# First spectrum step ahead of the ctx square sums, and adaLN blocks 11 to 15 mixed one k step later

## The chip, the cores and the metric

The kernel runs on one core of a Trainium2 chip. The metric is the device time of one execution in microseconds. "Before" is the kernel as it stands, "after" the kernel with the change. Engines are named as in the profile: PE is TensorE (PEld its weight loads), ACT is ScalarE, DVE is VectorE, POOL is GpSimd and SP is SyncE. SP and POOL issue transfers from queues of their own.

## The reference

One layer of a hybrid backbone over 512 latent tokens and 256 context tokens of 2048 channels. Only its first part matters here:

```
mod  = silu(c)     @ w_ada + b_ada     # 6 x 2048, the first 4096 columns are shift and scale of the mixer
modc = silu(c_ctx) @ w_ada + b_ada
h_x  = rms_norm(x + pos, g) * (1 + scale) + shift        # latents
h_c  = rms_norm(ctx, g) * (1 + cscale) + cshift          # context
u_c  = h_c @ w_in[:, :1024]
p_x  = h_x @ w_in                                        # split into u, Hyena v/x0/x1, gates
taps = window * filter_mlp(positions)                    # 1024 channels, forward and backward
kf   = spectrum of taps                                  # used much later, by the long convolution
```

After it come the S5 scan, the long convolution, the gated merge, the output projections and a SwiGLU feed-forward layer, which the change doesn't touch.

## The kernel before

Tensors are stored with channels on the 128 partitions, so that D = 2048 gives KT = 16 tiles of channels. Every engine has a program of its own, and semaphores order them. The order of work on each engine is written out by hand. The change concerns the first 180 us, in which four strands are interleaved.

**Coefficients (ada blocks 0 to 15).** Block c gives shift and scale of channel tile c, for x and for ctx. SP loads it (`ada_mix(c)` on SP, 2 MB, three buffers, so the load of block c waits for the end of the matmuls of block c - 3). PE multiplies it (`ada_mix(c)` on PE, 32 records of 128x256), ACT copies the result to SBUF (`ada_rows(c)`), PE turns the rows into columns (`mix_columns(c)`, four small matmuls), and DVE makes the coefficients (`mix_coefficients(c)`). PE's `ada_mix(c)` waits until DVE has the coefficients of block c - 2, since both use one of two PSUM banks.

**Norms.** ACT squares the ctx tiles and then the x tiles into four buffers (`square(k)`), and PE sums each with a matmul by ones (`sums(k)`), which frees the buffer. From the sums come the reciprocal roots `rs_x` and `rs_c`.

**Filter spectrum.** `taps(t)` makes four tiles of taps (PE, then DVE: s_tap counts finished tiles). Eight steps `spectrum_of_filter(st)` on PE (8 records of 128x512 each) are folded by DVE (`filter_fold(st)`, kf_free counts them) and stored to HBM by POOL. The fold of step st waits for the store of step st - 2.

**First products.** `weights(n)` on SP loads slice n of w_in (0.5 MB) into slot n % 3. ACT makes the high part (`split_hi(n)`), DVE the low part (`split_lo(n)`), and `units_by_k(k)` on PE does 24 matmuls for channel tile k with slice k // 2, into PSUM banks 0 to 5. It needs tile k of h, which DVE scales (`block(k)`: x, ctx, and the two low parts) and ACT completes (`h_hi_tile(k)`, `hc_hi_tile(k)`). Slot 1 lies over a buffer of the folds, so `weights(1)` waits for kf_free = 8, the last fold.

SP's queue is strict. Its order around the change is:

```
weights(0), ada_mix(11), weights(2), ada_mix(12), ada_mix(13), [kf_free 8] weights(1),
ada_mix(14), ada_mix(15), weights(3), weights(4), ...
```

After the 16 steps of `units_by_k` the kernel goes on with products for the other columns of w_in.

Of the kernel before, what the change touches and what calls it, by code (L numbers as in the profile page):

```python
# [22 lines left out]
KT = D // P  # L23
# [100 lines left out]
def block_kernel(nc, vecs_d, w_ac_d, w_ar_d, w_in_d, w_glu_d, w_hy_d, w_out_d, w_fi_d, w_fo_d, x_d, ctx_d,  # L124
# [363 lines left out]
    with nc.Block() as block:  # L488
# [375 lines left out]
        def _(act):  # L864
# [43 lines left out]
            def ada_rows(c):  # L908

                act.wait_ge(am_used, c + 1)  # L910
                act.activation(arow[c % 2][:, :], ps[6 + c % 2][:, 0:2 * P], ACT.Copy).then_inc(am_row, 1)
# [27 lines left out]
            for st in range(8):  # L939
                if 1 <= st < 5:  # L940
                    for k in range(KT + 4 * st - 4, KT + 4 * st):
                        square(k)
                if st == 4:
                    act.wait_ge(s_squ, 2 * KT)
                    act.activation(ssr[:, 0:SEQ], ps[4][:, :], ACT.Copy)
                    act.activation(ssr[:, SEQ:SEQ + CTX], ps[5][:, 0:CTX], ACT.Copy).then_inc(s_row, 1)
                if 2 <= st < 7:
                    ada_rows(3 + st)
                if st == 5:
                    act.wait_ge(s_var, 1)  # L950
                    act.activation(rt6[:, 2, :], rt6[:, 1, :], ACT.Sqrt).then_inc(s_sqrt, 1)
                if st == 6:
                    act.wait_ge(s_rsp, 1)
                    act.activation(rs_x[:, :], ps[5][:, :], ACT.Copy).then_inc(s_rs, 1)
                    act.activation(rs_c[:, :], ps[4][:, 0:CTX], ACT.Copy).then_inc(s_rs, 1)
                if st == 7:
                    h_hi_tile(0)
                    hc_hi_tile(0)
                    split_hi(0)
                    ada_rows(10)  # L960
                    ada_rows(11)
            for k in range(KT):
                if k < KT - 1:
                    h_hi_tile(k + 1)
                    hc_hi_tile(k + 1)
                if k == 0:
                    act.wait_ge(kf_free, 8)
                if k < 2:
                    split_hi(k + 1)
                if k < 4:  # L970
                    ada_rows(12 + k)
                if k >= 3 and k % 2 == 1:
                    split_hi(k // 2 + 2)

# [424 lines left out]
        def _(dve):  # L1399
# [36 lines left out]
            def position(k):  # L1436

                if k % 4 == 0:
                    dve.wait_ge(s_x[k // 4], 16)
                add_position(x_raw, postab, k).then_inc(s_xp, 1)  # L1440
# [29 lines left out]
            def mix_coefficients(c):  # L1470

                dve.wait_ge(am_cmb, c + 1)
                ins = tt(md[:, c, :], ps[6 + c % 2][:, 2 * P:2 * P + 4], vecs[:, V_B4 + 4 * c:V_B4 + 4 * c + 4], ADD)
                link(ins)
                ts(mu[:, c, :], md[:, c, 2:4], 1.0, vecs[:, V_NM + c:V_NM + c + 1], ADD, MUL).then_inc(c_mod, 1)
                dve.wait_ge(c_mod, c + 1)
# [28 lines left out]
            def filter_fold(st):  # L1505

                b = st % 2
                dve.wait_ge(kf_ps, st + 1)
                if st >= 2:
                    dve.wait_ge(kf_out[b], 16 * (st // 2))  # L1510
                even, odd = ps[2 * b][:, :], kf_odd[b][:, :]
                link(dve.tensor_copy(odd, ps[2 * b + 1][:, :]))
                tt(kfs[b][:, 0, :], even, odd, ADD)
                tt(kfs[b][:, 1, :], even, odd, SUB).then_inc(kf_free, 1)
# [8 lines left out]
            mix_coefficients(3)  # L1523
            for j in range(4):
                position(j)
            mix_coefficients(4)
            a, b, c, e, r = (rt6[:, j, :] for j in range(5))
            for st in range(8):
                if 1 <= st < 4:
                    for k in range(4 * st, 4 * st + 4):  # L1530
                        position(k)
                if st == 5:
                    dve.wait_ge(s_ss, 1)
                    link(ts(a, ps[4][:, 0:6], 1.0 / D, EPS, MUL, ADD))
                    dve.reciprocal(b, a).then_inc(s_var, 1)
                if st == 7:
                    dve.wait_ge(s_rs, 2)
                    block(0)
                    split_lo(0)
                filter_fold(st)  # L1540
                if st >= 3:
                    mix_coefficients(2 + st)
                if st == 5:
                    dve.wait_ge(s_sqrt, 1)
                    link(tt(e, c, c, MUL))
                    link(tt(e, e, a, MUL))
                    link(ts(e, e, -0.5, 1.5, MUL, ADD))
                    link(tt(r, e, c, MUL))
                    dve.wait_ge(s_id, 16)
                    for j in range(6):  # L1550
                        ts(dg[:, j, :], ident[:, :], rt6[:, 4, j:j + 1], None, MUL).then_inc(s_dg, 1)
            mix_coefficients(10)
            for k in range(KT):
                if k < KT - 1:
                    block(k + 1)
                if k == 0:
                    mix_coefficients(11)
                if 2 <= k < 6:
                    mix_coefficients(10 + k)
                if k < 2:  # L1560
                    split_lo(k + 1)
                if k >= 3 and k % 2 == 1:
                    split_lo(k // 2 + 2)
# [818 lines left out]
        def _(pe):  # L2382
# [18 lines left out]
            def sums(k):  # L2401

                pe.wait_ge(s_sq, k + 1)
                bank, w = (5, CTX) if k < KT else (4, SEQ)
                mm(ps[bank][32 * (k % 4):32 * (k % 4) + 1, 0:w], ones[:, 0:1], sqr[k % 4][:, 0:w], start=k % KT < 4,
                   stop=k % KT >= KT - 4, skip_group_check=True, tile_position=(0, 32 * (k % 4))).then_inc(s_squ, 1)
# [27 lines left out]
            def mix_columns(c):  # L2434

                pe.wait_ge(am_row, c + 1)
                for v in range(2):
                    ins = mm(ps[6 + c % 2][:, 2 * P + 2 * v:2 * P + 2 * v + 2], arow[c % 2][:, P * v:P * v + P],
                             vecs[:, V_SEL:V_SEL + 2], start=True, stop=True)
                ins.then_inc(am_cmb, 1)  # L2440

            def spectrum_of_filter(st):

                cs, f, half = 1 - st // 4, st // 2 % 2, st % 2
                if st % 4 == 0:
                    pe.wait_ge(s_tabf[cs], 16)
                if st >= 2:
                    pe.wait_ge(kf_free, st - 1)
                for t in range(4):
                    ins = mm(ps[2 * (st % 2) + t // 2][:, :], tab_f[cs][:, t, P * f:P * f + P],  # L2450
                             (taps_s, taps_d)[cs][:, t, 512 * half:512 * half + 512], start=t % 2 == 0, stop=t % 2 == 1)
                ins.then_inc(kf_ps, 1)
# [24 lines left out]
            taps(3)  # L2477
            mix_columns(3)
            ada_mix(4)
            for k in range(KT):  # L2480
                sums(k)
            mix_columns(4)
            pe.wait_ge(s_tap, 4)
            for st in range(8):
                if st == 5:
                    pe.wait_ge(s_row, 1)
                    for j in range(6):
                        ins = mm(ps[4][:, j:j + 1], ssr[:, P * j:P * j + P], vecs[:, V_SEL:V_SEL + 1], start=True, stop=True)
                    ins.then_inc(s_ss, 1)
                spectrum_of_filter(st)  # L2490
                if st >= 3:
                    mix_columns(2 + st)
                if 1 <= st < 5:
                    for k in range(KT + 4 * st - 4, KT + 4 * st):
                        sums(k)
                if st >= 2:
                    ada_mix(3 + st)
                if st == 6:
                    for j in range(6):
                        pe.wait_ge(s_dg, j + 1)  # L2500
                        out = ps[5][:, P * j:P * j + P] if j < 4 else ps[4][:, P * (j - 4):P * (j - 4) + P]
                        ins = mm(out, ones[:, :], dg[:, j, :], start=True, stop=True)
                    ins.then_inc(s_rsp, 1)
# [17 lines left out]
                if k % 2:  # L2521
                    ins.then_inc(w_used, 1)

            ada_mix(11)
            mix_columns(10)
            pe.wait_ge(kf_free, 7)
            for k in range(KT):
                units_by_k(k)
                if k < 5:
                    mix_columns(11 + k)  # L2530
                if k < 4:
                    ada_mix(12 + k)

            def half_unit(n, out, xh, xl, k0, first, last, nk=ST, each=None):

# [238 lines left out]
            for j in range(4):  # L2774
                n = N_HU + j
                pe.wait_ge(w_lo, n + 1)
                for kk in range(4):
                    k = 4 * j + kk
# [14 lines left out]
            for j in range(4):  # L2793
                n = N_HU + 4 + j
                pe.wait_ge(w_lo, n + 1)
                for kk in range(4):
                    i = 4 * j + kk
                    k = K_ORDER[i]
# [288 lines left out]
```

## Time and profile before

| | |
|---|---|
| median of 3 runs | 2776.26 us (2775.99 to 2779.75) |
| profiled execution | 2771.29 us, span 2769.5 us |
| PE busy in the span | 2726.0 us (98%) |
| DVE, ACT, POOL busy | 2170.0, 1138.4, 367.6 us |
| moved by DMA | 475.27 MB, mean 172 GB/s |
| span, 0 to 140 us | PE busy 116.7 us of 140 |

The busy time of PE is modelled from pipelined matmuls, so it shows where PE is idle, not that it is at its peak. Times in the rows below are microseconds from the start of the span.

### The profile page before, as it was taken

What the parts mean: (1) busy time and instruction counts of PE and PEld (TensorE: products, weight loads), DVE (VectorE), ACT (ScalarE), POOL (GpSimd) and SP (SyncE); (2) the same over time, 40 slices, a digit from 0 to 9 for tenths busy, and PEclk for the clock granted to TensorE, in tenths of its full rate; (3) what the DMA queues carried; (4) which work ended last, traced back from release to release, by engine and by line L of the source; (5) the groups of instructions that cost most, each with busy time, mean ns of one, the idle gap of its engine ahead of it and who ended that gap; (6) DMA issues with size and microseconds to landing.
All of it is one profiled execution on the core that took longest, in us unless ns stands there. A gap on an engine that the chain in (4) does not pass through costs nothing.

```text
span 2769.5 us, 39538 instructions
## 1 busy us (share of the span) xinstructions
PE 2726.0 (98%) x15566; PEld 2312.1 (83%) x15566; DVE 2170.0 (78%) x2984; ACT 1138.4 (41%) x1697; POOL 367.6 (13%) x540
## 2 busy tenths in 40 slices
PE   7999999999999999999999999999999999999997
PEld 2688888887888888888888888888888888998996
DVE  6556676987785686676789999999999887877877
ACT  4332333223443532222245555555555554453541
POOL 0001331001333100011100111111111111000001
PEclk9999999999999999999999999999999999999999
DMA  9736884336776645767644444444443336434432
GB/s 403 324 98 157 193 188 140 121 122 197 224 224 185 238 137 184 243 210 268 232 147 146 155 145 152 142 152 147 148 154 123 126 111 218 139 91 148 138 104 95
DMA packets 144540, 475.27 MB, mean 172 GB/s; under 512 B 24993, under 2 KB 29489, under 8 KB 140130
## 3 DMA queue, kind: packets, MB, share of 16 engines
q1 hardware_dynamic: 85858, 301.43, 33.2%
q0 software_dynamic: 49760, 157.67, 18.0%
q10 hardware_dynamic: 8736, 13.63, 1.4%
q8 instruction: 124, 2.03, 0.3%
q14 instruction: 62, 0.51, 0.1%
HBM read 428.14 MB, written 44.44 MB: 171 GB/s over the span
## 4 chain that ended last, share of the span: by engine, by line
PE 90%; DMA 5%; DVE 3%; ACT 2%; issue 1%; POOL 0%; ACTq 0%; SPq 0%; DVEq 0%; POOLq 0%
PE ps L2837 19%; PE ps L2541 12%; PE ps L2543 11%; PE ps L2542 11%; PE ps L2839 10%; PE ps L2887 3%; PE ps L2888 3%; PE ps L2886 3%; PE ps L2865 2%; PE ps L2866 2%; PE ps L2867 2%; PE ps L2558 2%; PE ps L2518 1%; DMA hw_raw<-in_w_in 1%; DMA kf<-kf_st 1%; PE ps L2585 1%
## 5 line engine op out<-in xcount | busy, mean ns | idle before, releaser
L1408 DVE TENSOR_TENSOR hw_lo<-hw_raw,hw_hi 128x1024 fp32r<-128x1024 f32 x220 | 269.2, 1224 | 316.3 <-ACT hw_hi L868 315.3
L868 ACT ACTIVATE hw_hi<-hw_raw 128x1024 fp32r<-128x1024 f32 x220 | 232.6, 1059 | 672.8 <-DMA hw_raw<-in_w_in 456.4
L2837 PE MATMUL ps<-t_hi_lo,wx_hi 128*128 128x512 f32 x1312 | 412.4, 396 | 0.0
L2107 DVE TENSOR_TENSOR wx_lo<-wx,wx_hi 128x1024 fp32r<-128x1024 f32 x287 | 351.5, 1225 | 41.4 <-ACT wx_hi L1262 36.9
L2541 PE MATMUL ps<-h_hi,hw_hi 128*128 128x512 f32 x896 | 354.2, 395 | 0.2 <-DVE st_c L1672 0.2
L2543 PE MATMUL ps<-h_hi,hw_lo 128*128 128x512 f32 x896 | 349.6, 390 | 0.0
L2542 PE MATMUL ps<-h_lo,hw_hi 128*128 128x512 f32 x896 | 349.0, 389 | 0.0
L1262 ACT ACTIVATE wx_hi<-wx 128x1024 fp32r<-128x1024 f32 x287 | 302.3, 1053 | 105.3 <-PE ps L2839 99.4
L2837 PE MATMUL ps<-h_hi_lo,wx_hi 128*128 128x512 f32 x984 | 309.3, 396 | 0.0
L2839 PEld LDWEIGHTS ps<-t_hi_lo,wx_lo 128*128 128x128 f32 x1312 | 246.8, 188 | 57.8
L2839 PE MATMUL ps<-t_hi_lo,wx_lo 128*128 128x256 f32 x1312 | 257.8, 278 | 0.0
L2839 PEld LDWEIGHTS ps<-h_hi_lo,wx_lo 128*128 128x128 f32 x984 | 185.1, 188 | 43.3
L1311 ACT ACTIVATE dw_hi<-dw 128x768 fp32r<-128x768 f32 (+1 forms) x192 | 144.4, 753 | 160.4 <-PE ps L2867 129.4
L2837 PEld LDWEIGHTS ps<-t_hi_lo,wx_hi 128*128 128x128 f32 x1312 | 199.7, 189 | 0.0
L2161 DVE TENSOR_TENSOR dw_lo<-dw,dw_hi 128x768 fp32r<-128x768 f32 (+1 forms) x192 | 162.0, 845 | 47.6 <-ACT dw_hi L1311 46.7
L2541 PEld LDWEIGHTS ps<-h_hi,hw_hi 128*128 128x128 f32 x896 | 168.3, 188 | 36.5 <-issue 2.2
L2543 PEld LDWEIGHTS ps<-h_hi,hw_lo 128*128 128x128 f32 x896 | 168.2, 188 | 35.7
L2542 PEld LDWEIGHTS ps<-h_lo,hw_hi 128*128 128x128 f32 x896 | 168.4, 188 | 33.7
L2839 PE MATMUL ps<-h_hi_lo,wx_lo 128*128 128x256 f32 x984 | 193.3, 278 | 0.0
L2888 PE MATMUL ps<-blk_lo_hi,dw_lo 128*128 128x256 f32 x672 | 190.4, 283 | 0.0
L2887 PE MATMUL ps<-blk_lo_hi,dw_hi 128*128 128x256 f32 x672 | 190.4, 283 | 0.0
L2886 PE MATMUL ps<-blk_lo_hi,dw_hi 128*128 128x256 f32 x672 | 190.3, 283 | 0.0
(429 smaller groups left out, 5667.0 us busy)
## 6 DMA issues: line engine op xcount, KB each, us to landing
wx<-in_w_fi SPq DMA_DIRECT2D x164, 512.0 KB, 3.5
hw_raw<-in_w_in SPq DMA_DIRECT2D x128, 512.0 KB, 4.6
ada1m<-in_w_ar POOLq DMA_DIRECT2D x96, 512.0 KB, 4.5
ada_mix<-in_w_ac SPq DMA_DIRECT2D x16, 2048.0 KB, 12.8
dw<-in_w_fo SPq DMA_DIRECT2D x80, 384.0 KB, 3.1
ada1g<-in_w_ar POOLq DMA_DIRECT2D x32, 512.0 KB, 5.5
hw_raw<-in_w_glu SPq DMA_DIRECT2D x32, 512.0 KB, 4.7
hw_raw<-in_w_out SPq DMA_DIRECT2D x32, 512.0 KB, 4.4
```

The lines of the kernel that those rows point to most:

```text
L868: act.activation(hw_hi[slot(n)][:, :], hw_raw[slot(n)][:, :], ACT.Copy).then_inc(w_hi, 1)
L1262: act.activation(wx_hi[o % 4][:, :], wx[x_buffer(p, j)][:, :], ACT.Copy).then_inc(w_hi, 1)
L1408: tt(hw_lo[s][:, :], hw_raw[s][:, :], hw_hi[s][:, :].bitcast(F32), SUB).then_inc(w_lo, 1)
L2107: tt(wx_lo[b][:, :], wx[b][:, :], wx_hi[o % 4][:, :].bitcast(F32), SUB).then_inc(w_lo, 1)
L2541: mm(out, wh(k), xh[:, k0 + k, :], start=first and k == 0, stop=False)
L2542: mm(out, wh(k), xl[:, k0 + k, :], start=False, stop=False)
L2543: ins = mm(out, wl(k), xh[:, k0 + k, :], start=False, stop=last and k == nk - 1)
L2837: mm(out[:, :], wh[:, P * k:P * k + P], both[:, :, k, :], start=opens and k == 0, stop=False, skip_group_check=True)
L2839: ins = mm(out[:, 0:CW], wl[:, P * k:P * k + P], xh[:, k, :], start=False, stop=k == ST - 1, skip_group_check=True)
L2886: mm(out, wh[:, w], b_hi[j][:, k, :], start=opens and k == 0, stop=False, skip_group_check=True)
L2887: mm(out, wh[:, w], b_lo[j][:, k, :], start=False, stop=False, skip_group_check=True)
L2888: ins = mm(out, wl[:, w], b_hi[j][:, k, :], start=False, stop=k == K_S - 1, skip_group_check=True)
```

## The change

On PE, `spectrum_of_filter(0)` now comes ahead of the sixteen `sums(k)` of ctx and of `mix_columns(4)`. On DVE, `filter_fold(0)` comes ahead of `mix_coefficients(4)` and of the loop over the steps.

The sequence of ada blocks in the loop over k moves. Before, PE did `ada_mix(11)` and `mix_columns(10)` ahead of the loop, then after step k the columns of block 11 + k and the product of block 12 + k. Now columns 10 follow step 0, columns 9 + k follow steps 2 to 6, and the product of block 10 + k follows steps 1 to 5, so that block 11 comes behind units 1 and block 15 behind units 5. ACT's `ada_rows` and DVE's `mix_coefficients` move with them. The program of SP is unchanged, but its loads of blocks 14 and 15 wait for the ends of the products of blocks 11 and 12.

```
# ACT
                     split_hi(0)
                     ada_rows(10)
-                    ada_rows(11)
             for k in range(KT):
...
-                if k < 4:
-                    ada_rows(12 + k)
+                if 2 <= k < 7:
+                    ada_rows(9 + k)
                 if k >= 3 and k % 2 == 1:
                     split_hi(k // 2 + 2)
# DVE
             for j in range(4):
                 position(j)
+            filter_fold(0)
             mix_coefficients(4)
...
-                filter_fold(st)
+                if st:
+                    filter_fold(st)
...
-            mix_coefficients(10)
             for k in range(KT):
                 if k < KT - 1:
                     block(k + 1)
-                if k == 0:
-                    mix_coefficients(11)
-                if 2 <= k < 6:
-                    mix_coefficients(10 + k)
+                if k == 1:
+                    mix_coefficients(10)
+                if 3 <= k < 8:
+                    mix_coefficients(8 + k)
                 if k < 2:
                     split_lo(k + 1)
# PE
             ada_mix(4)
-            for k in range(KT):
-                sums(k)
-            mix_columns(4)
             pe.wait_ge(s_tap, 4)
             for st in range(8):
...
                 spectrum_of_filter(st)
+                if st == 0:
+                    for k in range(KT):
+                        sums(k)
+                    mix_columns(4)
...
-            ada_mix(11)
-            mix_columns(10)
             pe.wait_ge(kf_free, 7)
             for k in range(KT):
                 units_by_k(k)
-                if k < 5:
-                    mix_columns(11 + k)
-                if k < 4:
-                    ada_mix(12 + k)
+                if k == 0:
+                    mix_columns(10)
+                if 2 <= k < 7:
+                    mix_columns(9 + k)
+                if 1 <= k < 6:
+                    ada_mix(10 + k)
```

## Rows read from the trace of the kernel before

**Rows 1.** The page: busy time, share of the span, instructions.

```profile
PE 2726.0 (98%) x15566; PEld 2312.1 (83%) x15566; DVE 2170.0 (78%) x2984; ACT 1138.4 (41%) x1697; POOL 367.6 (13%) x540
```

**Rows 2.** Windows: stretch, length, busy by engine, PE clock, DMA share, GB/s.

```profile
59.00:111.10 52.10, 49.90 (x416) 27.11 (x415) 27.39 (x62) 13.70 (x27) 5.01 (x7) 1.00 1.01 426
...
120.00:138.00 18.00, 17.22 (x147) 13.43 (x146) 9.24 (x22) 5.92 (x10) 1.10 (x2) 1.00 0.16 55
```

**Rows 3.** The chain of waits, 96 to 117 us: start, length, what.

```profile
98.34 0.61 DVE kf_st L1514
98.96 12.12 DMA hw_raw<-in_w_in
111.16 1.07 ACT hw_hi L868
...
116.29 0.47 PE ps L2518
```

**Rows 4.** SP's issues, 90 to 113 us (x2: first issue to second).

```profile
90.19 7.48 SPq L499 DMA_DIRECT2D ada_mix<-in_w_ac  x2
98.96 0.33 SPq L509 DMA_DIRECT2D hw_raw<-in_w_in  x1
101.38 7.39 SPq L499 DMA_DIRECT2D ada_mix<-in_w_ac  x2
112.84 0.33 SPq L509 DMA_DIRECT2D hw_raw<-in_w_in  x1
```

**Rows 5.** PE in order of time, 99 to 135 us (idle before, its releaser).

```profile
99.41 1.91 PE L2429 MATMUL ps<-ada_mix,silu_c 128*2 128x256 f32 x32 [2.13 <-DVE mul_mix L1475]
...
101.72 0.48 PE L2518 MATMUL ps<-h_hi,hw_hi 128*128 128x512 f32 x1
...
106.05 0.50 PE L2438 MATMUL ps<-vecs,ada_row 128*128 128x2 f32 x4
...
108.31 0.51 PE L2518 MATMUL ps<-h_hi,hw_hi 128*128 128x512 f32 x1
...
116.29 0.47 PE L2518 MATMUL ps<-h_hi,hw_hi 128*128 128x512 f32 x1 [1.30 <-DVE hc_lo L1496]
...
122.81 0.50 PE L2518 MATMUL ps<-h_hi,hw_hi 128*128 128x512 f32 x1
...
134.90 0.47 PE L2518 MATMUL ps<-h_hi,hw_hi 128*128 128x512 f32 x1 [0.78 <-DVE hc_lo L1496]
```

**Rows 6.** Tile views: ada block issued at 97.34, then slice issued at 139.3.

```profile
DMA to landing us min/median/max: 12.5/12.5/12.5
...
DMA to landing us min/median/max: 3.7/3.7/3.7
```

**Rows 7.** PE and DVE in order of time, 41 to 57 us.

```profile
42.93 5.83 PE L2405 MATMUL ps<-sqr,ones 128*1 128x256 f32 x32 [3.45 <-ACT sqr L898]
49.16 7.11 PE L2450 MATMUL ps<-taps_dif,tab_f 128*128 128x512 f32 x16
...
41.72 0.68 DVE L1459 TENSOR_TENSOR taps_dif<-window,window 128x512 f32<-128x512 f32 x1
```

**Rows 8.** PE's clock: windows (clock third from last), then tap matmuls.

```profile
43.43:46.00 2.57, 2.57 (x16) 0.60 (x14) 0.99 (x2) 2.41 (x8) 0.00 (x0) 0.50 0.99 414
...
46.50:48.50 2.00, 2.00 (x15) 0.51 (x12) 1.01 (x2) 2.00 (x8) 0.00 (x0) 1.00 0.98 410
...
14.61 3.78 PE L2417 MATMUL ps<-f3w,fh 64*128 64x512 f32 x8 [5.22 <-ACT fh L884]
...
21.04 1.99 PE L2417 MATMUL ps<-f3w,fh 64*128 64x512 f32 x8 [0.41 <-DVE window L1448]
```

**Rows 9.** Slice 3's split to the coefficients behind it: the chain, then DVE.

```profile
129.87 0.96 ACT hw_hi L868
...
134.36 0.41 DVE hc_lo L1496
...
134.86 0.23 DVE L1475 TENSOR_SCALAR mul_mix<-mod_mix,vecs 128x2 f32<-128x2 f32 x1
```

## The prediction

> **What bounds the kernel now.** I read the page first. TensorE is busy for 98% of the span [rows 1], so most of the program is bound by it, and a change in the first 150 us pays only if it lets TensorE reach the long dense part sooner; after 140 us its idle time is small waits on neighbours, none on a clock of its own, so I pass any shift on to the end in full. Next I read the first 140 us by stretches. From 59 to 111 us all 16 DMA engines are full (share 1.01, 426 GB/s); from 120 to 138 us they are nearly empty (0.16) [rows 2]. So this stage has two limits, a DMA one until about 111 us and a TensorE one behind it. The chain of waits shows where they meet: the fold of the last spectrum step ends at 98.95, weight slice 1 is issued at 98.96, lands 12.12 us later at 111.1, and through its split on ACT and DVE and the scaling of the third h tile it releases units_by_k(2) at 116.29 [rows 3]. Last I read SP's issues [rows 4] and TensorE's order [rows 5] around that point.
>
> **Why slice 1 lands when it does.** SP issues ada block 13 at 97.34 (the second of the pair that begins at 90.19), slice 1 at 98.96 [rows 4]. Block 13 lands 12.5 us after its issue, at 109.8; slice 1 lands 1.3 us later [rows 3, 6], which is its own 0.52 MB at 426 GB/s (1.2 us). It was therefore not waiting for its issue but for the bytes ahead of it. Whoever issues it a microsecond or two sooner only lengthens its time in the queue.
>
> **Edit 1, spectrum step 0 ahead of the 16 sums of ctx squares.** TensorE reaches this place at 39.48 and waits 3.45 us for the first square [rows 7]. Step 0 needs the fourth tap tile, whose last subtraction ends on DVE at 42.40 [rows 7]. So the wait does not go; it ends 0.4 us sooner, on DVE. Step 0 takes 3.56 us (7.11 for two, rows 7) and ends at 46.0. Only four square buffers exist, so ACT squares four tiles and then stands until the sums start; the other twelve go at the present pace, 5.83/16 = 0.36 us each [rows 7], to 50.4. With its columns step 1 then starts near 51.5 in place of 52.7: 1.2 us sooner. If the low clock seen in this place [rows 8] catches step 0, it lasts up to 1.8 us longer and the gain is a loss of up to 0.6 us. Folds 0 and 1 and their stores to HBM move 2 to 6 us forward, which takes away DVE's waits for the stores; those bytes must be moved all the same before slice 1 lands. So either way ada_mix(10) ends between 96.1 and 97.9 instead of 97.28, and slice 1 is issued between 97.7 and 99.5, while block 13 is still ahead of it. Value of edit 1: nothing, covered by the full DMA engines. Were they not full it would be worth its 1.2 us.
>
> **Edit 2, ada blocks 11 to 15 one or more k steps later.** Before the first units TensorE now waits 2.13 us for the coefficients of block 9, then does ada_mix(11) and mix_columns(10) [rows 5]. Both leave, so units_by_k(0) starts near 96.1 rather than 101.72. A step of units takes 4.33 us, one mix_columns with one ada_mix 2.26 us (106.05 to 108.31), a whole round 6.52 us (116.29 to 122.81) [rows 5]. New order: units 0 to 100.4, mix_columns(10), units 1 to 105.2, ada_mix(11) to 107.1 (108.9 if step 0 was slow). Then units 2 stands until slice 1 is there. In DVE's queue the block for tile 2 still stands behind the low part of slice 1, and both follow its landing as now: 116.3. The 5 us won ahead become a wait of 7 to 9 us.
>
> What then follows is longer. Before 116.3 the kernel now has ada_mix(12) and (13) done; the new one has them still to do. **Term 1**: two rounds of 2.26 us, 4.5 us more behind the wait. The 0.78 us wait before units 5 at 134.90 [rows 5] has ACT standing at ada_row 15 ahead of the split of slice 3; that order goes, so minus 0.8. Term 1 is 3.7 us.
>
> **Term 2, the queues it is moved past.** SP's order is block 14, block 15, slice 3. Block 15's load waits for the end of ada_mix(12), because there are three buffers; now it goes out at 108.4 (with block 14 in the 101.38 row) and slice 3 at 112.84, long before it is needed [rows 4]. In the new order ada_mix(12) ends only after units 2; call that moment T (122.8 at full clock). At T block 15 goes out (2.1 MB), then slice 3. A slice alone lands in 3.7 us [rows 6]; block 15 ahead of it adds 2.1 MB / 426 GB/s = 4.9 us. I take slice 3 at T + 8.7 us. Units 3, columns 12, ada_mix(13), units 4 keep TensorE until T + 6.5 + 4.3 = T + 10.8. What follows is mix_columns(13), which waits for ada_row 13, queued on ACT behind the split of slice 3 and h_hi of tile 5; and ada_mix(14), which waits for coefficient 12, queued on DVE behind the low part of slice 3 and tile 5's block. Now, from the start of such a split (129.87) to the end of the coefficients behind the block (134.86 + 0.23) it is 5.2 us [rows 9]. So ada_mix(14) starts at T + 8.7 + 5.2 + 0.1 = T + 14.0 and units 5 at T + 15.9; without the wait T + 13.0. Term 2 is 2.9 us. Bounds: nothing if slice 3 came 3 us sooner; 4.5 us if the pair shares the engines badly (now, behind other loads, slice 1 took 12.1, three more than I give slice 3).
>
> The Trainium skill, "DMA: Bandwidth & Descriptors", section "Anatomy of one DMA — SWDGE (gpsimd) path", fits one DMA as about 2.0 us plus its bytes at 436 GB/s, for issues from GpSimd. By it slice 3 would land at about T + 8.0, term 2 would be 2.2 us and the whole sum 7.8. The row of a lone slice on this queue (3.7 us, of which its bytes are 1.2) shows 2.5 us fixed, and I go by the row.
>
> **Term 3, the clock.** An idle TensorE for 3.45 us at 39.5 was followed by a granted clock of 0.50 from 43.4 to 46.0 and 1.00 from 46.5 [rows 8], that is 1.2 and then 2.4 GHz. What the lower level costs is seen in the tap matmuls: eight of them took 3.78 us after 5.2 us idle and 1.99 us later [rows 8], 1.8 us lost. The new wait of 7 to 9 us is longer than both, units 2 is dense work behind it, so I put 1.9 us; from nothing (the 2.13 us and 1.30 us waits of rows 5 lowered nothing) to 3.7 us, twice the tap row, if it stays low for longer or falls again in the wait of term 2.
>
> **Sum.** 3.7 + 2.9 + 1.9 = 8.5 us. The profiled execution took 2771.29 us, its span 2769.5; with the change 2779.8. The median of the runs stands 5.0 us above the profiled one, at 2776.26, so I predict 2784.8 us, 0.31% slower. Below 0.2% (5.6 us) a difference is what a measurement of this kernel can't tell from none.
>
> **Rivals.**
> (a) Only term 1: the clock stays or recovers at once and slice 3 comes in time. 2776.3 + 3.7 = 2780.0, no change that counts. For it: the 2.13 us wait left the clock alone, DMA is empty by T. Against it: the long wait is four times that one.
> (b) Faster: slice 1 is bound by its issue and by the stores, not by the queue. With folds and stores 2 to 6 us sooner it would land sooner, and TensorE would run dense from 51.5 on: 1.2 + 2.13 + 1.30 + 0.78 = 5.4 us less, 2770.9. Its place is the landing of slice 1. Units 2 can follow ada_mix(11) at 107.1 only if slice 1 lands at 102; to be even with the present kernel it has to come about 7 us sooner, by 104, since terms 1 and 2 stay. For it: the chain of waits does run through the stores and the folds. Against it: block 13 is ahead of it and the engines were full all the way [rows 2, 6].
> (c) Worse: slice 3 late by its upper bound and a clock that falls twice, 3.7 + 4.5 + 3.7 = 11.9 us, 2788.2.
>
> **Numbers.** Forecast 0.70, rival (a) 0.15, (b) 0.07, (c) 0.08. The likeliest case's own range is 5.6 to 11 us, 2781.9 to 2787.3. To hold 8 in 10 I reach down to (a) less 1 us and up to (c), as the runs themselves lie between 2775.99 and 2779.75: 2779.0 to 2788.5. Slower 0.78 (forecast and (c)), within 0.2% 0.15, faster 0.07.
>
> **What the new profile would show.** Spectrum step 0 released by DVE's tap at 42.4, not by ACT. Units 0 near 96 to 98. A TensorE idle of 7 to 9 us ended by the hc_lo of tile 2 near 116, the landing of slice 1 within a microsecond of 111, granted clock 0.5 behind it. Slice 3 issued near 123 to 125 in place of 112.8, and a second idle of 2 to 3 us before mix_columns(13) or ada_mix(14). The last units step ending 8 to 9 us later than now. The prediction is wrong if slice 1 lands well before 108, if the second wait is missing, or if a later part of the kernel takes the 8 us back.

## The result, and the profile after

The changed kernel takes 2787.95 us (median of 6 runs, 2785.46 to 2790.32) against 2776.25 us before (6 runs). The ratio is 1.0036, with a 95% interval of 1.0026 to 1.0046: 0.36% slower, 11.7 us between the medians. The predicted 2784.8 us is 3.2 us short of it. The measured time lies within the range of 2779.0 to 2788.5, but near its upper end, above the likeliest case's own 2781.9 to 2787.3.

The profiled execution of the changed kernel has a span of 2786.3 us, 16.8 us over that of before. The first stage accounts for 12.2 of them. I read its end off the first matmul of the products behind the sixteen steps of units, first before and then after (PE in order of time):

```profile
180.74 0.39 PE L2558 MATMUL ps<-h_hi,hw_hi 128*128 128x512 f32 x1
```

```profile
192.91 0.39 PE L2559 MATMUL ps<-h_hi,hw_hi 128*128 128x512 f32 x1
```

Most of the other 4.6 us lies between 1000 and 1500 us. The waits there, from the view of who waited for whom, first before and then after:

```profile
PE ps L2769 <- DVE hw_lo L1408: 2.1, 2, 1.5
PE ps L2541 <- DVE hw_lo L1408: 0.6, 2, 0.4
```

```profile
PE ps L2542 <- DVE hw_lo L1407: 3.0, 7, 1.2
PE ps L2770 <- DVE hw_lo L1407: 2.1, 2, 1.5
PE ps L2542 <- DVE xacc L1955: 1.0, 2, 0.8
```

These are 2.7 us before and 6.1 after, but 7.3, 5.1 and 5.3 us in the profiles of e1, e2 and e8 below, which the change touches in part or in another form. So their number varies between executions whatever the edit. The profiled execution of before had few of them, and was 5.0 us faster than its own median. So spans are a poor measure of this change; below I read the end of the stage, and the medians of the runs beside it.

The first stage of the changed kernel. The chain of waits up to the wait of PE, to be held beside [rows 3]:

```profile
98.59 0.61 DVE kf_st L1513
99.22 13.18 DMA hw_raw<-in_w_in
112.48 1.06 ACT hw_hi L868
...
117.54 0.77 PE ps L2519
```

SP's issues, beside [rows 4]:

```profile
90.65 7.48 SPq L499 DMA_DIRECT2D ada_mix<-in_w_ac  x2
99.22 0.33 SPq L509 DMA_DIRECT2D hw_raw<-in_w_in  x1
108.70 17.53 SPq L499 DMA_DIRECT2D ada_mix<-in_w_ac  x2
126.28 4.35 SPq L509 DMA_DIRECT2D hw_raw<-in_w_in  x2
```

PE in order of time, beside [rows 5] and [rows 7]:

```profile
42.55 5.40 PE L2450 MATMUL ps<-taps_dif,tab_f 128*128 128x512 f32 x8 [3.05 <-DVE taps_dif L1458]
...
97.67 0.50 PE L2519 MATMUL ps<-h_hi,hw_hi 128*128 128x512 f32 x1
...
106.73 1.91 PE L2429 MATMUL ps<-ada_mix,silu_c 128*2 128x256 f32 x32
...
117.54 0.77 PE L2519 MATMUL ps<-h_hi,hw_hi 128*128 128x512 f32 x1 [8.90 <-DVE hc_lo L1495]
123.50 0.50 PE L2438 MATMUL ps<-vecs,ada_row 128*128 128x2 f32 x4
123.93 1.91 PE L2429 MATMUL ps<-ada_mix,silu_c 128*2 128x256 f32 x32
...
130.10 0.50 PE L2438 MATMUL ps<-vecs,ada_row 128*128 128x2 f32 x4
...
139.71 0.61 PE L2438 MATMUL ps<-vecs,ada_row 128*128 128x2 f32 x4 [2.83 <-ACT ada_row L911]
140.65 2.65 PE L2429 MATMUL ps<-ada_mix,silu_c 128*2 128x256 f32 x32 [0.34 <-DVE mul_mix L1474]
...
148.40 0.50 PE L2438 MATMUL ps<-vecs,ada_row 128*128 128x2 f32 x4
```

Windows (PE clock third from last, then DMA share and GB/s), beside [rows 2] and [rows 8]:

```profile
59.00:111.10 52.10, 49.64 (x391) 27.27 (x389) 26.24 (x58) 14.05 (x28) 5.01 (x7) 1.00 1.01 419
117.50:121.00 3.50, 3.46 (x11) 3.02 (x12) 3.07 (x5) 1.37 (x4) 0.00 (x0) 0.50 0.00 0
121.00:123.00 2.00, 2.00 (x12) 1.74 (x11) 1.65 (x4) 0.79 (x3) 0.00 (x0) 0.95 0.00 0
140.65:145.00 4.35, 4.35 (x37) 2.47 (x38) 2.48 (x6) 2.45 (x4) 0.00 (x0) 0.62 0.02 4
145.00:148.00 3.00, 3.00 (x18) 2.54 (x18) 2.47 (x4) 0.94 (x2) 0.00 (x0) 0.98 0.01 3
```

What to see: units 0 starts at 97.67 in place of 101.72, four microseconds sooner, and all of it and more is lost in the 8.90 us in which PE waits for tile 2, which hangs on slice 1. Slice 1 was issued at 99.22, 0.26 us later than before, and landed at 112.4. Units 2 then runs at a granted clock of 0.50 for its first 3.5 us. Slice 3 goes out at 126.28 in place of 112.84, and a second wait of 2.83 and 0.34 us follows, again with the low clock behind it.

The second wait in the chain of waits of the changed kernel:

```profile
126.28 8.88 DMA hw_raw<-in_w_in
135.18 1.07 ACT hw_hi L868
...
139.78 0.40 DVE hc_lo L1495
...
140.28 0.24 DVE mul_mix L1474
...
140.65 2.65 PE ps L2429 x32
```

### The profile page after: what moved, and what is told of

It reads as the page before. It is cut to its first block, busy times and chain, and to the rows that moved or that the text cites. A ratio compares the mean times of both kernels' runs of the same rounds, so it can differ in the third digit from the quotient of the medians.

```text
span 2786.3 us, 39538 instructions
## 1 busy us (share of the span) xinstructions
PE 2731.9 (98%) x15566; PEld 2312.4 (83%) x15566; DVE 2169.8 (78%) x2984; ACT 1138.1 (41%) x1697; POOL 367.5 (13%) x540
## 4 chain that ended last, share of the span: by engine, by line
PE 89%; DMA 4%; DVE 4%; ACT 2%; issue 1%; POOL 0%; ACTq 0%; SPq 0%; DVEq 0%; POOLq 0%
PE ps L2838 19%; PE ps L2542 11%; PE ps L2544 11%; PE ps L2543 11%; PE ps L2840 10%; PE ps L2889 3%; PE ps L2888 3%; PE ps L2887 3%; PE ps L2866 2%; PE ps L2868 2%; PE ps L2867 2%; DMA hw_raw<-in_w_in 2%; PE ps L2559 2%; PE ps L2519 1%; PE ps L2450 1%; DMA hw_raw<-in_w_glu 1%
```

## The experiments

"Stage end" is the start of the first matmul behind the sixteen units steps, 180.7 us before and 192.9 in the changed kernel. Ratios are to before, from runs on the same chip; they are estimated over the single runs and can differ by a few hundredths of a per cent from the quotient of two medians.

| kernel | units 2 starts | stage end | median us | ratio (95%) |
|---|---|---|---|---|
| before | 116.29 | 180.74 | 2776.25 | |
| changed | 117.54 | 192.91 | 2787.95 | 1.0036 (1.0026 to 1.0046) |
| e1, edit 1 alone | 116.14 | 180.66 | 2776.03 | 1.0002 (0.9993 to 1.0011) |
| e2, edit 2 alone | 115.99 | 191.52 | 2787.14 | 1.0041 (1.0027 to 1.0055) |
| e3, changed, slice 3 ahead | 116.35 | 186.64 | 2781.62 | 1.0018 (1.0009 to 1.0027) |
| e4, changed, slice 1 ahead | 111.83 | 188.53 | 2781.35 | 1.0017 (1.0008 to 1.0027) |
| e5, before, slice 1 ahead | 115.53 | 180.14 | 2777.19 | 1.0002 (0.9993 to 1.0011) |
| e6, changed, both ahead | 111.41 | 182.22 | 2777.26 | 1.0000 (0.9991 to 1.0009) |
| e7, changed, wait filled | 115.98 | 190.49 | 2785.07 (one) | |
| e8, rebuilt | 111.29 | 177.64 | 2773.01 | 0.9987 (0.9978 to 0.9996) |
| e9, e8 with SP's old order | 116.53 | 185.50 | 2780.74 | 1.0008 (0.9998 to 1.0017) |
| e10, e8 with edit 1 | 112.00 | 178.65 | 2774.05 | 0.9988 (0.9979 to 0.9997) |

### e1 and e2: each edit alone

e1 is the kernel before with this part of the change; e2 is the changed kernel without it.

```
# DVE
+            filter_fold(0)
             mix_coefficients(4)
# PE
-            for k in range(KT):
-                sums(k)
-            mix_columns(4)
...
                 spectrum_of_filter(st)
+                if st == 0:
+                    for k in range(KT):
+                        sums(k)
+                    mix_columns(4)
```

> The kernel before with edit 1 alone (spectrum step 0 and its fold ahead of the ctx square sums). My theory: slice 1 is bound by the bytes ahead of it in the full DMA engines, so units step 2 starts within 1.3 us of 116.3 and the last units step ends within 1.5 us of the 180.7 of before; time within 0.1% of before (2774.5 to 2778). Rival (the edit pays where slice 1 is bound by its issue): units step 2 at 115 or sooner and 1 to 3 us less. Rival (edit 1 is itself part of the loss, as slice 1 landed 1.3 us later in the changed kernel): 1 to 2 us more.

> The changed kernel with edit 1 undone, so edit 2 alone. My theory: edit 2 is the whole loss; slice 1 lands near 111 to 112.4, units step 2 starts at 116.3 to 117.5 after an idle of 7 to 9 us, the first matmul of the columns after the units steps starts 11 to 12.5 us later than the 180.7 of before; time 2786 to 2789. Rival (both edits are needed for the loss): 6 us more than before or less.

Edit 1 is worth nothing: stage end 180.66 against 180.74. Its chain of waits shows slice 1 as it was:

```profile
98.87 12.06 DMA hw_raw<-in_w_in
111.00 1.07 ACT hw_hi L868
```

The folds and stores in between did move forward: POOL issues the store of step 0 at 49.95 in place of 55.27 and that of step 2 at 63.60 in place of 68.84. But step 0 ran at the low clock and took 5.12 us, and the last fold, and with it the issue of slice 1, stayed where it was (98.87 against 98.96). So e1 shows that edit 1 is worth nothing, but not yet what a sooner issue would have brought; e4 to e6 show that.

Edit 2 alone is the loss: stage end 191.52, ratio 1.0041. PE in order of time in e2:

```profile
115.99 0.77 PE L2516 MATMUL ps<-h_hi,hw_hi 128*128 128x512 f32 x1 [7.54 <-DVE hc_lo L1495]
```

The stage ends 10.8 us later than before, a little under the 11 to 12.5 expected. The rivals to these two expectations fall. Units 2 starts at 116.14 and 115.99, so the 117.54 of the changed kernel's profile is not the work of edit 1, nor of the two edits together, since e3 and e7 below contain both and have 116.35 and 115.98. In that execution DMA seems to have been behind from the beginning: DVE's first work on the x tiles, which waits for their load, starts at 46.33 in place of 45.01 (44.81 in e1, 44.62 in e2). Why is not shown.

### e3: slice 3 ahead of block 15

```
# SP
-            for c in range(14, KT):
-                ada_mix(c)
-            weights(3)
+            ada_mix(14)
+            weights(3)
+            ada_mix(15)
```

> The changed kernel with slice 3 of w_in issued ahead of the load of ada block 15. It tests term 2: slice 3 is then issued before 110 and ready long before it is needed, so the second wait (2.8 + 0.3 us) and the low clock behind it go. My theory: the units steps end 4.5 to 5.5 us sooner than in the changed kernel (192.9), near 188, and the time is 2783 to 2784. Rival (the wait for row 13 is only taken over by the next one, such as the load of block 15): less than 2 us sooner.

SP issues slice 3 at 108.86, and PE goes through the place of the second wait without one (PE in order of time):

```profile
129.13 0.50 PE L2438 MATMUL ps<-vecs,ada_row 128*128 128x2 f32 x4
129.56 1.91 PE L2429 MATMUL ps<-ada_mix,silu_c 128*2 128x256 f32 x32
135.67 0.50 PE L2438 MATMUL ps<-vecs,ada_row 128*128 128x2 f32 x4
136.10 1.91 PE L2429 MATMUL ps<-ada_mix,silu_c 128*2 128x256 f32 x32
142.21 0.50 PE L2438 MATMUL ps<-vecs,ada_row 128*128 128x2 f32 x4
```

A round is 6.54 us here, twice. In the changed kernel the same two rounds took 9.61 (130.10 to 139.71) and 8.69 us (139.71 to 148.40), so the second wait and the clock behind it cost 3.07 + 2.15 = 5.2 us. The stage ends 6.3 us sooner, 1.2 of it because units 2 started sooner in this execution; the other 5.1 are within the 4.5 to 5.5 expected. The median is 2781.62 us, below the 2783 to 2784 expected.

### e4, e5 and e6: slice 1 ahead of block 13

```
# SP
-            ada_mix(13)
             sp.wait_ge(kf_free, 8)
             weights(1)
+            ada_mix(13)
```

e4 has it on the changed kernel, e5 on the kernel before, and e6 is e4 with the edit of e3.

> The changed kernel with slice 1 issued ahead of the load of ada block 13; block 13 then waits for the last fold too, at about 99.2. It tests whether slice 1 waits for bytes ahead of it. My theory: issued at the same 99.2, slice 1 lands about 5 us sooner (2.1 MB at 426 GB/s), near 107.5, units step 2 starts near 112.6, the units steps end 4 to 5 us sooner than in the changed kernel, and the time is 2783 to 2784. Rival (slice 1 is bound by its issue and a fixed latency): it lands 13 us after its issue as before, and nothing changes.

> The kernel before with slice 1 issued ahead of the load of ada block 13. My theory: slice 1 lands near 107 in place of 111.1, after which TensorE itself sets the start of units step 2, near 115 (block 13's product then ends just before); the wait of 1.30 us goes, and the units steps end about 1.3 us sooner than 180.7, a difference that the times can't show. Rival (block 13, now loaded last, is late for its product at 113): no gain or 1 to 2 us more.

> The changed kernel with both moves of SP: slice 1 ahead of block 13 and slice 3 ahead of block 15. My theory: the two gains are of different waits and add up, 4.4 us and 5 us from 192.9, so the units steps end near 183 to 184, still later than the 180.7 of before by the two rounds of blocks and the low clock less the wait saved; time 2778 to 2780. Rival (one wait hides the other): 186 or later.

The chain of waits of e4:

```profile
97.86 8.83 DMA hw_raw<-in_w_in
106.77 1.06 ACT hw_hi L868
...
111.83 0.77 PE ps L2519
```

Slice 1 takes 8.83 us from its issue in place of 13.18, because the 2.1 MB of block 13 are behind it and no longer ahead. It lands at 106.7, where e2, e3 and e7 have 110.8 to 111.2 with block 13 ahead. The issue itself also came 1.36 us sooner than in the changed kernel (97.86 against 99.22), because spectrum step 0 ran at the full clock in this execution (3.70 us, not 5.40) and the last fold ended sooner. The same holds for e6:

```profile
97.73 8.54 DMA hw_raw<-in_w_in
```

So e4 and e6 are the test of why edit 1 pays nothing. In them it did bring its 1.2 us: slice 1 is issued 1.1 and 1.2 us sooner than before had it (98.96). But it lands no sooner for that. The five executions with slice 1 ahead of block 13 issue it at 97.73 (e6), 97.86 (e4), 99.20 (e10), 99.58 (e5) and 99.75 (e8), and it lands at 106.3, 106.7, 106.8, 107.3 and 106.1.

In e5 it lands 7.7 us after its issue and PE no longer waits for tile 2. The stage ends 0.6 us sooner in place of the 1.3 expected, as that execution had been 0.6 us behind before this place (its ada_mix(11) starts at 100.03, against 99.41 in [rows 5]). In e6 the two gains add up, 182.22, a little better than expected. (The 192.91 that both are counted from holds the 1.2 us by which units 2 was late in that one execution. Held against e2's 191.52, e4's own gain in the stage end is 3.0 us; the round behind its second wait took 9.29 us in place of 8.69.) The medians of e4 and e6, 2781.35 and 2777.26 us, are 0.7 to 1.7 us below what was expected. The changed order on the compute engines with a better order on SP is thus level with before (1.0000), not better: PE still stood 4.2 us ahead of units 2, which then took 6.48 us.

### e7: the wait filled

The changed kernel with 32 extra matmuls whose results nobody reads.

```
# PE, in the loop over k
+                if k == 1:
+                    pe.wait_ge(c_mod, 10)
+                    for j in range(32):
+                        mm(ps[7][:, 3 * P:4 * P], ones[:, :], ones[:, :], start=True, stop=True, skip_group_check=True)
                 if 1 <= k < 6:
                     ada_mix(10 + k)
```

> The changed kernel with 32 extra matmuls of 128x128 between units step 1 and the product of block 11, results unused: they fill most of the wait for slice 1. It tests the clock. My theory: units step 2 starts at the same 116 to 117.5 but runs at 2.4 GHz, 4.25 us in place of 5.96, so everything behind is 1.7 us sooner; the second wait and its low clock stay. Rival (units step 2 was slow for another cause): it still takes about 6 us.

PE in order of time, then a window over units 2:

```profile
115.98 0.47 PE L2519 MATMUL ps<-h_hi,hw_hi 128*128 128x512 f32 x1 [0.16 <-DVE hc_lo L1495]
...
120.22 0.50 PE L2438 MATMUL ps<-vecs,ada_row 128*128 128x2 f32 x4
```

```profile
116.00:120.00 4.00, 4.00 (x23) 3.52 (x24) 3.57 (x7) 1.39 (x4) 0.00 (x0) 1.00 0.83 254
```

Units 2 takes 4.24 us at a granted clock of 1.00. In the changed kernel it takes 5.96, the first 3.5 us of them at 0.50. That is 1.7 us, as expected. That everything behind would be 1.7 us sooner was a miss. From units 2 to the end of the stage it is 74.5 us against 75.4, 0.9 less, since the round behind the second wait took 9.45 us here (columns at 136.53 and 145.98) and not 8.69. The clock stayed low for longer there, as a window shows:

```profile
136.53:142.00 5.47, 5.47 (x39) 2.83 (x40) 3.36 (x10) 1.99 (x4) 0.00 (x0) 0.50 0.00 0
```

ada_mix(14) took 3.59 us, against 2.65 in the changed kernel and 1.91 at the full clock.

### e8, e9 and e10: a rebuilt order

The experiments point to a version in which slice 1 comes early, slice 3 comes early, and PE has enough to do until slice 1 is there. Relative to the kernel before:

```
# SP: the edits of e3 and e4
# ACT
-                    ada_rows(11)
             for k in range(KT):
...
+                if k < 5:
+                    ada_rows(11 + k)
                 if k == 0:
                     act.wait_ge(kf_free, 8)
...
-                if k < 4:
-                    ada_rows(12 + k)
# DVE
-            mix_coefficients(10)
...
-                if k == 0:
-                    mix_coefficients(11)
-                if 2 <= k < 6:
+                if k < 6:
                     mix_coefficients(10 + k)
# PE
-            ada_mix(11)
-            mix_columns(10)
...
                 units_by_k(k)
-                if k < 5:
-                    mix_columns(11 + k)
-                if k < 4:
-                    ada_mix(12 + k)
+                if k < 6:
+                    mix_columns(10 + k)
+                if k < 5:
+                    ada_mix(11 + k)
```

e9 is e8 with SP's order of before, e10 is e8 with edit 1.

> A version meant to beat both: the kernel before with ada blocks 11 to 15 half a step later than before and one step earlier than in the change (columns 10 + k behind step k, product 11 + k behind step k), slice 1 ahead of block 13, slice 3 ahead of block 15. My theory: no 2.13 us wait, units step 2 near 112 to 113 after a wait under 3 us that leaves the clock alone, three rounds behind it in place of two, no second wait; the units steps end near 178, 2 to 3 us sooner than before, 0.1% of the time, so the times alone will hardly show it. Rival (the wait for slice 1 lowers the clock, or rows on ACT delay the splits): 180 or later.

> The rebuilt order of the ada blocks with SP's order of before (slice 1 behind block 13, slice 3 behind block 15). It tests whether the gain of the rebuilt version lies in SP's order or in the order on TensorE. My theory: slice 1 lands near 111 again and units step 2 starts near 116.3 after a wait of 4 to 5 us; three rounds of blocks behind it in place of two, and the low clock behind a wait of that length (1.7 to 2.2 us): the units steps end near 184, 3 us later than before. Rival (the order on TensorE is the gain): 180 or sooner.

> The rebuilt version with edit 1 added. It tests whether edit 1 pays once slice 1 no longer stands behind block 13. My theory: no; TensorE comes 0 to 1.2 us sooner to units step 2, which slice 1 releases at the same time, so the units steps end within 0.5 us of the rebuilt version's, 177.6. Rival: 176.5 or sooner.

The chain of waits of e8, then PE in order of time at the same place:

```profile
99.75 6.32 DMA hw_raw<-in_w_in
...
106.16 1.07 ACT hw_hi L868
...
111.29 0.47 PE ps L2514
```

```profile
111.29 0.47 PE L2514 MATMUL ps<-h_hi,hw_hi 128*128 128x512 f32 x1 [0.27 <-DVE hc_lo L1495]
```

Slice 1 is there at 106.1 and PE waits 0.27 us for it. The stage ends at 177.64, 3.1 us sooner than before, and the median is 2773.01 us against 2777.01 of before on the same chip: ratio 0.9987, 0.9978 to 0.9996. It beats both kernels: before by 0.13%, the changed one by 0.5% (by their ratios to before). e9 shows that the gain needs SP's order: with the old one PE waits 6.53 us at the same place, longer than the 4 to 5 expected, and the stage ends at 185.50 (184 expected). Slice 1 ahead alone, on the order of before (e5), brought 0.6 us of the 3.1. Which part of the rest belongs to slice 3's move was not tested: no run has it on the order of before, or the rebuilt order without it. e10 shows no gain from edit 1 here either: the stage ends 1.0 us later, twice the expected bound, of which 0.7 is there at the start of units 2 (112.00). The ratios of the two, 0.9988 and 0.9987, don't differ.

## Why the prediction was right

**What bounds the stage.** Right. The 59 to 111 us stretch has the DMA engines at 1.01 in the changed kernel too, and e4 moves slice 1's landing by 4 to 5 us by changing only what is ahead of it. The Trainium skill says in "DMA: Bandwidth & Descriptors", section "Issuing engines are not separate DMA queues", that transfers from all issuing engines run on the same 16 engines and interleave. The trace of before agrees. From 30 to 100 us SP's queue (q1) and POOL's (q0) share the 16 engines' time; together they leave nothing of it, and move 425 GB/s (packets, MB, share of the 16 engines):

```profile
q1 hardware_dynamic: 2406, 26.18, 88.4%
q0 software_dynamic: 939, 3.45, 12.1%
```

**Edit 1, nothing.** Right. Step 0 was released by DVE's tap at 42.55 in the changed kernel. It took 5.40 us, the low-clock case that the text had beside the 3.56; ada_mix(10) ended at 97.7, within the 96.1 to 97.9. With that clock there was no gain left to be covered: slice 1 was issued no sooner than before. That the full engines cover it where it is there was shown only by e4 and e6, whose 1.1 to 1.2 us sooner issue brought no sooner landing.

**Term 1, two rounds more less the 0.78 us wait, 3.7 us.** Right; e3's rounds of 6.54 us match [rows 5], and the 0.78 us wait is gone.

**Term 2, slice 3 behind block 15, 2.9 us.** Right in mechanism, a little small. ada_mix(12) ended at 125.8 and slice 3 landed at 135.2, T + 9.3 against T + 8.7; the wait was about 3.5 us. By the fit of the Trainium skill's "DMA: Bandwidth & Descriptors", section "Anatomy of one DMA — SWDGE (gpsimd) path", the estimate was T + 8.0, so the lone slice's row was the better guide, and still short by 0.6.

**Term 3, the clock, 1.9 us.** The size that was off. The first low stretch cost 1.7 us (5.96 against 4.24 us in e7). But the clock also fell in the second wait, which the prediction had only as an upper bound and in rival (c): of the 5.2 us that e3 measured there, 3.5 are the wait and about 1.7 the clock, seen in ada_mix(14)'s 2.65 us for 1.91 and in units 5 behind it. Term 3 measured 3.4.

**The sum.** From units 2 to the stage end, before took 64.45 us and after 75.37: 10.9 more, against 8.5 predicted. 3.7 + 1.7 + 5.2 = 10.6; the missing 0.3 I did not follow. The start of units 2 was 1.25 us later in this execution, which the other profiles don't repeat. The 8.5 grew by the second low stretch (1.7) and term 2 (0.6). The shift was passed on to the end: 10.8 us in e2's stage and 10 to 12 us in the medians.

**Rivals.** (a) falls with the changed kernel's own trace: slice 3 didn't come in time and the clock fell; e3 and e7 price both. (b) falls. Earlier folds and stores left slice 1 where it was in e1, and where its issue did come sooner, in e4 and e6, it landed no sooner. Its other half was sound, as a slice 1 that lands sooner does pay (e4). (c) came nearest in the time, 2788.2 against the 2787.95 measured. It had the second fall of the clock right. Its upper bounds were too high by 1.0 us for slice 3 (4.5 against 3.5) and 0.3 for the clock (3.7 against 3.4), and 1.2 of the measured 12.2 us of the stage was the late start of units 2 in one execution. So the terms of the forecast and their order were right; the clock's second fall, which its sum left out, stood only in this rival, with a chance of 0.08.

## What to carry to other kernels

Where transfers fill the engines, as here, an operand lands when the bytes ahead of it are through, not when it is issued. Compute that freed its issue 1.2 us earlier gained nothing, and one swapped line in the queue let units 2 start 4 to 5 us sooner (111.4 and 111.8 in e4 and e6, 116.0 to 116.4 in e2, e3 and e7). Work that lies in front of a wait is free there and costs its full time behind it: moving it back past the wait moves it onto the path. And follow each moved product to the load that waits for it and to whatever is queued behind that load, here a weight slice that was needed sooner than the block ahead of it.

## What the runs showed that I had not expected

A wait of about 3 us on TensorE can go either way for its clock. PE in order of time at spectrum step 0, in e1 and in e4:

```profile
42.47 5.12 PE L2452 MATMUL ps<-taps_dif,tab_f 128*128 128x512 f32 x8 [3.05 <-DVE taps_dif L1459]
```

```profile
42.83 3.70 PE L2450 MATMUL ps<-taps_dif,tab_f 128*128 128x512 f32 x8 [3.05 <-DVE taps_dif L1458]
```

The changed kernel, e7 and e10 are like e1 (5.40 us), and so is e3 (5.21 us behind a wait of 2.85); e6 is like e4. What decides between the two is not shown. The 2.13 us wait of [rows 5] left the clock alone, but the second wait of the changed kernel (2.83 us, four short matmuls, 0.34 us) was followed by the low clock. For waits of this length a prediction should carry both outcomes. The Trainium skill, "TensorE: Matmul & The Clock Gate", section "What's actually happening", describes a low level at 1.2 GHz when idle and 2.4 GHz after activity. The traces agree: windows in which the clock doesn't change show 0.50 or 1.00.

Nor is the price of a fall fixed. Units 2 took 5.9 to 6.5 us behind the long wait in e2, e3, e4, e6, e9 and the changed kernel, against 4.24 at the full clock, and the second fall cost from about 1.7 us (the changed kernel) to 2.9 us (e7, a round of 9.45 us against 6.54).
